# Two rounds of a crowded expert pair, merged tile by tile

## The reference

```python
def hierarchical_moe(h, w_grp, w_exp, w1, w3, w2):
    # t: 256 tokens x 1024
    # top-1 of 4 groups, then top-2 of that group's 4 experts, with weights
    gate = jnp.sum(jax.nn.one_hot(expert, N_EXPERTS, ...) * e_w[..., None], axis=1)
    hg = jnp.einsum('td,edf->tef', t, w1)
    hu = jnp.einsum('td,edf->tef', t, w3)
    a = jax.nn.silu(hg) * hu * gate[..., None].astype(t.dtype)
    y = jnp.einsum('tef,efd->td', a, w2)
```

## Time and profile before

| | |
|---|---|
| median of three executions | 819.1 us |
| the profiled execution: its own time | 825.06 us |
| its span, first to last instruction | 823.3 us |
| TensorE busy | 763.1 us (93%) |
| VectorE, ScalarE, GpSimd busy | 234.7, 165.1, 50.1 us |
| moved by DMA, mean over the span | 289.66 MB, 352 GB/s |
| mean granted TensorE clock | 0.95 of full speed |

### The profile page before, as it was taken

One profiled execution on the slowest core, in us unless ns is written; L12 is line 12 of the kernel. 1 busy time (PEld: TensorE's weight loads), 2 busy tenths in 40 slices (PEclk: granted clock), 3 DMA queues, 4 the chain that ended last, 5 costly groups with the idle time before them and its releaser, 6 DMA issues.

```text
span 823.3 us, 10418 instructions
## 1 busy us (share of the span) xinstructions
PE 763.1 (93%) x4039; PEld 428.6 (52%) x4039; DVE 234.7 (29%) x666; ACT 165.1 (20%) x372; POOL 50.1 (6%) x74
## 2 busy tenths in 40 slices
PE   4799879999999999999899999999997989999796
PEld 4287458764344433443588758683334333333344
DVE  2301331441112111110679931451211112111115
ACT  3120330331000110011503852451000000110012
POOL 5013000010000000000100000001000000001000
PEclk9899999869999999999999999959997999999988
DMA  9996999969999999999997359567999909999941
GB/s 290 400 398 238 413 409 429 361 270 378 425 427 426 425 429 428 425 427 416 399 402 275 112 223 427 195 267 317 431 427 422 398 9 414 426 427 424 424 190 55
DMA packets 42640, 289.66 MB, mean 352 GB/s; under 512 B 4417, under 2 KB 5901, under 8 KB 30290
## 3 DMA queue, kind: packets, MB, share of 16 engines
q1 hardware_dynamic: 36752, 275.78, 81.9%
q0 software_dynamic: 5056, 11.98, 3.9%
q10 hardware_dynamic: 770, 1.06, 0.4%
HBM read 285.63 MB, written 8.52 MB: 357 GB/s over the span
## 4 chain that ended last, share of the span: by engine, by line
PE 79%; DMA 13%; DVE 3%; issue 3%; ACT 1%; POOL 1%; SPq 0%; DVEq 0%; POOLq 0%
PE ps L518 75%; DMA ring<-in_w_ada 6%; DMA ring<-in_conv_w 4%; DMA back<-in_moe_w 4%; DVE work L1753 1%; PE ps L944 1%; PE ps L809 1%; PE ps L742 1%; PE ps L780 0%; DVE rstd L1490 0%; POOL work L1371 0%; PE ps L670 0%; DVE back L1954 0%; PE ps L1064 0%; ACT back L1137 0%
## 5 line engine op out<-in xcount | busy, mean ns | idle before, releaser
L518 PE MATMUL ps<-ring,work 128*64 128x512 f32 x1088 | 306.2, 596 | 2.0 <-DMA back<-in_moe_w 1.1
L518 PEld LDWEIGHTS ps<-ring,work 128*64 128x64 f32 x1088 | 95.0, 137 | 144.1 <-issue 143.8
L518 PE MATMUL ps<-back,ring 128*128 128x256 f32 x656 | 147.4, 386 | 4.3 <-ACT back L1137 3.1
L518 PEld LDWEIGHTS ps<-back,ring 128*128 128x128 f32 x656 | 126.2, 194 | 24.7 <-issue 4.2
L518 PE MATMUL ps<-bench,work 128*64 128x512 f32 x208 | 97.5, 618 | 3.4 <-issue 3.3
L518 PE MATMUL ps<-spare,work 128*64 128x512 f32 x176 | 80.1, 609 | 4.7 <-issue 4.7
L518 PE MATMUL ps<-back,work 128*64 128x512 f32 x160 | 72.0, 596 | 0.0
L1753 DVE TENSOR_TENSOR work<-work,ps 128x256 f32<-128x256 f32 x34 | 19.4, 613 | 161.7 <-PE ps L518 161.7
L518 PE MATMUL ps<-ring,csil 128*32 128x512 f32 x352 | 45.7, 649 | 8.5 <-DMA ring<-in_w_ada 8.5
L1203 ACT ACTIVATE work<-ps 128x512 f32<-128x512 f32 x17 | 10.1, 597 | 210.1 <-PE ps L518 210.1
L1918 DVE SCALAR_TENSOR_TENSOR work<-work,dw 128x256 f32<-128x256 f32 x120 | 50.9, 485 | 1.0
(11 more groups left out here) (238 smaller groups left out, 640.2 us busy)
## 6 DMA issues: line engine op xcount, KB each, us to landing
ring<-in_moe_w SPq DMA_DIRECT2D x63, 2048.0 KB, 19.4
ring<-in_w_ada SPq DMA_DIRECT2D x22, 2048.0 KB, 17.8
bench<-in_moe_w SPq DMA_DIRECT2D x12, 2048.0 KB, 20.3
spare<-in_moe_w SPq DMA_DIRECT2D x11, 2048.0 KB, 20.2
back<-in_moe_w SPq DMA_DIRECT2D x10, 2048.0 KB, 21.2
ring<-in_conv_w SPq DMA_DIRECT2D x6, 2048.0 KB, 24.4
ring<-in_w_in_ab SPq DMA_DIRECT2D x2, 2048.0 KB, 25.0
ring<-in_w_out_ab SPq DMA_DIRECT2D x2, 2048.0 KB, 23.1
```

What stands on the lines that cost most here:

```text
L518: return nc.tensor.matmul(out, lhsT, rhs, start=start, stop=stop, skip_group_check=True)
```

## The change

For a crowded pair of kind 1, the last pair of a layer excepted, the three engines run a new function `both` in the block behind the program. It walks the tiles once: w1 for round 0 (bank 6) and for round 1 (bank 4), then w3 for round 1 (bank 5) and for round 0 (bank 7). The two w1 tiles are given back behind the first product of w3, the two w3 tiles behind round 1's transposes; then come w2 of round 1, the transposes of round 0, the scatter of round 1, the next pair's token rows, and w2 of round 0, behind which w2's tiles are given back. Round 1 has its own scatter matrix, `spread_more`. At the end the engines jump to the next pair (`pe_next`) instead of into the middle of this one; the usual code of the pair is skipped. The usual code now ends with the jump to `pe_next`, where it had one to `pe_round` before it. VectorE's `compact` is split into helpers (`take_spread`, `choose_next`, `gated_rows`, `turned_high`, `give_high`) with the same instructions in the same order. The waits on `ysel_lo`, `ysel_hi`, `hsel_lo` and `hsel_hi` stand behind the second reading of `path` instead of ahead of it. The core of the diff (TensorE, then ScalarE's and VectorE's `both`):

```diff
+        spread_more = work[:, 46 * P:48 * P]
...
+def both(l, i):
+    n = i + l * PAIRS
+    w1, w3, w2 = experts_of(l, i)
+    chosen = (hsel, hsel_more)
+    pe.wait_ge(ysel_lo[0], n)
+    pe.wait_ge(ysel_hi[0], n)
+    pe.wait_ge(hsel_lo[0], n + 1)
+    pe.wait_ge(hsel_hi[0], n + 1)
+    pe.wait_ge(more_ready, n + 1)
+    gather(1, i, 0)
+    gather(1, i, 1)
+    tile_landed(l, i, 0)
+    tile_landed(l, i, 1)
+    pe.wait_ge(mod_taken, (6, 9)[l])
+    for r, bank in ((0, 6), (1, 4)):
+        pe.wait_ge(hsel_lo[r], n + 1)
+        for k in range(DC):
+            if k == 4:
+                pe.wait_ge(hsel_hi[r], n + 1)
+                pe.wait_ge(pick_ready[r], n + 1)
+                if r:
+                    pe.wait_ge(spread_ready[0], n + 1)
+                for g in range(2):
+                    if is_sent(l, i, r):
+                        last = mm(ps[:, 7, 0:4].rearrange("p (s u) -> p s u", s=2), pick[i % 2][:, g, :],
+                                  send[:, g, :, 2 * i:2 * i + 2], g == 0, g == 1)
+                    else:
+                        last = nc.tensor.transpose(ps[:, 7, g * TG:(g + 1) * TG], pick_gate[:, g, :], ident)
+                last.then_inc(spread_done[r], 1)
+            for u in range(2):
+                c = slice(CAP * u, CAP * u + CAP)
+                last = mm(ps[c, bank, :], chosen[r][:, k, c], w1[u][:, k, :], k == 0, k == DC - 1)
+        last.then_inc(hid_done[r], 1)
+    tile_landed(l, i, 2)
+    tile_landed(l, i, 3)
+    for r, bank in ((1, 5), (0, 7)):
+        if r == 0:
+            pe.wait_ge(spread_ready[1], n + 1)
+        for k in range(DC):
+            for u in range(2):
+                c = slice(CAP * u, CAP * u + CAP)
+                last = mm(ps[c, bank, :], chosen[r][:, k, c], w3[u][:, k, :], k == 0, k == DC - 1)
+            if k == 0 and r:
+                pe.wait_ge(hid_done[1], n * 2 + 1)
+                pe.sem_inc(tiles_used, 2)
+        last.then_inc(hid_done[r], 1)
+    def turn(r, bank):
+        for f in range(FC):
+            if f % 2 == 0:
+                pe.wait_ge(hid_ready[r], n * 2 + (f // 2 + 1))
+            last = nc.tensor.transpose(ps[:, bank + f // 2, (f % 2) * P:(f % 2 + 1) * P],
+                                       hid[:, f * P:(f + 1) * P], ident)
+            if f % 2:
+                last.then_inc(turn_done[r], 1)
+    def outer(r):
+        for h in range(2):
+            if r == 0:
+                pe.wait_ge((hsel_lo, hsel_hi)[h][0], n + 2)
+            for f in range(FC):
+                if h == 0 and f % 2 == 0:
+                    pe.wait_ge((hidT_lo[r], hidT_hi[r])[f // 2], n + 1)
+                for u in range(2):
+                    c = slice(CAP * u, CAP * u + CAP)
+                    last = mm(ps[c, 4 + h, :], hidT[:, f, c], w2[u][:, f, h * 512:(h + 1) * 512],
+                              f == 0, f == FC - 1)
+            if h == 0 or not is_sent(l, i, r):
+                last.then_inc(ysel_done[r], 1)
+            else:
+                last.then_inc(tiles_used, 2)
+    def scatter(r, rows):
+        pe.wait_ge(ysel_lo[r], n + 1)
+        for m in range(DC):
+            if m == 4:
+                pe.wait_ge(ysel_hi[r], n + 1)
+            last = mm(psx[:, m, :], ysel[:, m * P:(m + 1) * P], rows, False, True)
+            if m == 0 and r == 0:
+                pe.wait_ge(ysel_done[r], ysel_count(l, i, r) + 2)
+                pe.sem_inc(tiles_used, 2)
+        last.then_inc(round_done[r], 1)
+    turn(1, 4)
+    pe.wait_ge(hid_done[0], n * 2 + 2)
+    pe.sem_inc(tiles_used, 2)
+    tile_landed(l, i, 4)
+    tile_landed(l, i, 5)
+    outer(1)
+    turn(0, 6)
+    pe.wait_ge(y_zeroed, l + 1)
+    scatter(1, spread_more)
+    pe.wait_ge(rows_in, 16 * (i + l * FETCHED + 1))
+    turn_rows(0)
+    if i + 2 < PAIRS:
+        locate(l, i + 2, ps[:, 5, 0:1])
+    pe.wait_ge(at_ready, min(i + 2, FETCHED) + l * FETCHED)
+    turn_rows(1)
+    outer(0)
+    if not is_sent(l, i, 0):
+        scatter(0, spread)
...
         way = pe.value_load(path[0:1, i:i + 1], min_val=0, max_val=2)
         with pe.If(way == 1):
-            pe.wait_ge(more_ready, n + 1)
-            gather(1, i, 0)
-            gather(1, i, 1)
-            compact(l, i, 1)
+            if i + 1 < PAIRS:
+                both(l, i)
+            else:
+                pe.wait_ge(ysel_lo[0], n)
+                pe.wait_ge(ysel_hi[0], n)
+                pe.wait_ge(hsel_lo[0], n + 1)
+                pe.wait_ge(hsel_hi[0], n + 1)
+                pe.wait_ge(more_ready, n + 1)
+                gather(1, i, 0)
+                gather(1, i, 1)
+                compact(l, i, 1)
+                pe.wait_ge(pick_back, n + 1)
+                compact(l, i, 0)
 
             pe.sem_inc(gather_done[2], 2)
             pe.sem_inc(hperm_done, 1)
             pe.sem_inc(gatebc_done, 1)
             pe.sem_inc(dense_done, 2 * FC)
...
-        pe.wait_ge(pick_back, n + 1)
-        pe.wait_ge(hsel_lo[2], n + 1)
-        pe.wait_ge(hsel_hi[2], n + 1)
-        pe.br(f"pe_round_{n}")
+            pe.wait_ge(hsel_lo[2], n + 1)
+            pe.wait_ge(hsel_hi[2], n + 1)
+            compact(l, i, 0)
+        pe.br(f"pe_next_{n}")
...
-        pe.br(f"pe_round_{n}")
-        nc.switch_bb(f"pe_round_{n}", parent=pe_at[n])
         compact(l, i, 0)
+        pe.br(f"pe_next_{n}")
+        nc.switch_bb(f"pe_next_{n}", parent=pe_at[n])
...
+def both(l, i):
+    n = i + l * PAIRS
+    take_low(1, n)
+    act.wait_ge(hid_done[1], n * 2 + 1)
+    nc.scalar.activation(sil, ps[:, 4, :], ACT.Silu).then_inc(sil_ready[1], 1)
+    act.wait_ge(turn_done[1], n * 2 + 1)
+    nc.scalar.activation(hidT[:, 0:2, :], ps[:, 4, 0:2 * P].rearrange("p (f j) -> p f j", f=2),
+                         ACT.Copy).then_inc(hidT_lo[1], 1)
+    act.wait_ge(hid_done[0], n * 2 + 1)
+    act.wait_ge(hid_ready[1], n * 2 + 2)
+    nc.scalar.activation(sil, ps[:, 6, :], ACT.Silu).then_inc(sil_ready[0], 1)
+    act.wait_ge(ysel_done[1], 2 * n + 1)
+    if l == 1:
+        act.wait_ge(y_sent, 16 * min(i, SENT))
+    nc.scalar.activation(ysel[:, 0:512], ps[:, 4, :], ACT.Copy).then_inc(ysel_lo[1], 1)
+    act.wait_ge(turn_done[0], n * 2 + 1)
+    nc.scalar.activation(hidT[:, 0:2, :], ps[:, 6, 0:2 * P].rearrange("p (f j) -> p f j", f=2),
+                         ACT.Copy).then_inc(hidT_lo[0], 1)
+    take_low(0, n + 1)
+    give_low(l, i, 0)
...
+def both(l, i):
+    n = i + l * PAIRS
+    take_high(1, n)
+    take_spread(l, i, 0, spread)
+    dve.wait_ge(more_ready, n + 1)
+    choose_gate(i, pick_ready[1], pick_more)
+    take_spread(l, i, 1, spread_more)
+    choose_next(l, i)
+    gated_rows(l, i, 1, 5)
+    turned_high(l, i, 1, 5)
+    gated_rows(l, i, 0, 7)
+    give_high(l, i, 1)
+    turned_high(l, i, 0, 7)
+    if i + 2 < PAIRS:
+        take_at(l, i + 2, ps[:, 5, 0:1])
+    take_high(0, n + 1)
+    give_high(l, i, 0)
+    dve.sem_inc(pick_back, 1)
```

More of the change, by code:

```diff
@@ L1241, in crowded @@
                     with act.If(way == 1):
-                        take_low(1, n)
-                        compact(l, i, 1)
+                        if i + 1 < PAIRS:
+                            both(l, i)
+                        else:
+                            take_low(1, n)
+                            compact(l, i, 1)
+                            compact(l, i, 0)
                         act.sem_inc(hsel_lo[2], 1)
@@ L1257, in crowded @@
                         take_low(2, n)
-                    act.br(f"act_round_{n}")
+                        compact(l, i, 0)
+                    act.br(f"act_next_{n}")
             def moe_act(l):
@@ L1717, in sum_sent, with take_spread @@
                                 ALU.add).then_inc(y_summed, 1)
-            def compact(l, i, r):
+            def take_spread(l, i, r, rows):
                 n = i + l * PAIRS
@@ L1736, in compact, with choose_next, gated_rows @@
                 else:
[L1737 to L1748, removed]
+                    V.tensor_copy(rows, ps[:, 7, 0:NT]).then_inc(spread_ready[r], 1)
+            def choose_next(l, i):
+                choose_gate(i + 1, pick_ready[0])
+                choose_more(l, i + 1)
+                if i + 2 < PAIRS:
+                    choose_pick(l, i + 2, 0, (picked[0], l * PAIRS + i + 3))
+            def gated_rows(l, i, r, bank):
+                n = i + l * PAIRS
                 dve.wait_ge(sil_ready[r], n + 1)
@@ L1754, in compact, with turned_high, give_high @@
                                     sil.rearrange("s (p f) -> s f p", f=FC)[:, f, :],
-                                    ps[:, 7, :].rearrange("s (p f) -> s f p", f=FC)[:, f, :],
+                                    ps[:, bank, :].rearrange("s (p f) -> s f p", f=FC)[:, f, :],
                                     ALU.mult).then_inc(hid_ready[r], 1)
[L1757 to L1760, removed]
+            def turned_high(l, i, r, bank):
+                n = i + l * PAIRS
                 dve.wait_ge(turn_done[r], n * 2 + 2)
```

(51 more changed lines are left out.)

15 lines of the change are left out of this document (7 added, 8 removed).

## The result

The changed kernel takes 808.38 us (median of four, 807.33 to 811.08); the kernel before, with a fourth execution beside it, 820.04. The ratio is 0.986 with a 95% interval of 0.983 to 0.989: 11.7 us less, where 8.5 were forecast, inside the range. A second comparison gave 0.9856 (0.9828 to 0.9883). The profiled execution of before was a long one (825.06; its other executions on record lie between 815.81 and 823.55), so the spans, 823.3 and 806.3, differ by more than the medians; 2.9 us of that had already arisen ahead of pair 3 (tile 26 goes out at 623.12 instead of 626.03).

A forecast was written before the change was run, and what follows sets the result against it. The weight stream, idle 18.1 us in pair 3, was taken to bound layer 1's end. Waits -6.7, clock -2.2 and TensorE's path +0.4 gave -8.5 us: 819.1 to 810.6, range 807 to 817.5.

The forecast's parts named there:

- Added: End of pair 3: jump into the next pair costs 3.31 + 1.7 us, plus 1.3 for reading `path` and a compare.
- TensorE's sum: TensorE's own path through crowded pair 3: 1.3 - 0.7 - 0.8 + 0.6 = +0.4 us, bounds -1.7 and +3.8.
- the entry: Jump into pair 3's far block: waits partly overlap the second reading of `path`, -0.7 us, at most 0.9.
- The 0.78 ahead of the transposes: Inside pair 3: round 1's transposes no longer wait for VectorE, since round 0's w3 stands between; -0.8 us.
- the new wait for `at_ready`: Right behind `locate` in pair 3: a bare trip to VectorE and back, 0 to 1.2 us, taken as +0.6.
- all three waits go: Pairs 6 and 7: TensorE's waits for tiles, 0.82, 1.14 and 4.71 us, vanish; 6.7 us, plus 2.2 of clock.
- TensorE bounds the rest: End of layer 1: tile 45 lands at 775.7, TensorE wants it at 776.8, so the stream delays nothing further.
- tile 33: Weight stream after pair 3: lands at 710.0, not 717.3; less than 5 us earlier would show the forecast wrong.
- that pass still waits over 2 us: Pair 7's w3 pass: no idle time expected before it; a wait over 2 us would show the forecast wrong.
- the dear exit: End of pair 3: exit costs 6.72 us plus a second stall of 1.85; TensorE loses 5.7, 815.9 us; chance 0.10.
- the late code: Inside `both`: TensorE stops twice more for code at 6.72 us each, 13.4 in all, 824.0 us; chance 0.07.
- shorter waits without a profiler: Last pairs' tile waits: unprofiled, only 2.9 of 8.9 us can go, 2.5 left, 816.6 us; chance 0.10.

The follow-up runs named there:

- the second experiment: Changed kernel with the four tiles of w1 and w3 given back only just ahead of round 0's w2 products: 821.6 us, ratio to before 1.0025.
- the drained kernel: Changed kernel with TensorE waiting for its own last w2 product before the jump to the next pair: 812.2 us, ratio to before 0.988.
- the reversed blocks: Kernel before with only the far blocks of all pairs laid out in reverse order: median 818.0 us, ratio 0.998; traced execution 813.65.
- the scatter last: Changed kernel with round 1's eight scatter products moved behind round 0's w2 products: 802.2 us, repeated 804.9; ratio to before 0.980.

## Why the prediction was right, and where it was not

The direction, the mechanism and the range held. The end of layer 1 was bound by the weight stream, and the gain is the standstill taken out of it: without the early give-backs nothing is left of it (the second experiment), and the time follows "26 to 45" through most of the table (not for the drained kernel, which was late by itself, nor for the reversed blocks, where the trace is not of a typical execution).

The step that failed is the one headed "Added": a jump at the end of the pair, "I price it equally, 3.31 + 1.7", with 1.3 on top. In the changed kernel these 6.3 us are not there. The row of before was read as the price of a jump wherever it stands; it was what was left of it with little work queued ahead. VectorE's copy that the last wait ahead of that jump is for:

```profile
661.65 0.69 DVE L1775 COPY work<-ps 128x512 f32<-128x512 f32 x1 [6.78 <-PE ps L518]
```

It ends at 662.34; the rest of the scatter, 2.8 us, runs behind it, and the next product starts at 668.50, 6.2 us after the copy. In the changed kernel the like copy ends at 676.18, and the products queued behind that wait last until pair 4 starts at 682.73, 6.5 us. Drained, the gap is 3.70 again. So the jump is hidden when enough products stand behind the last wait. How long it takes is not one number in these runs: 6.2 us from the wait in before, 4.6 in the same code with the blocks reversed, 3.70 behind the drain.

The rest of TensorE's sum: the entry was to win 0.7 by overlap and won nothing (3.54 against 3.56), but the gather took 632.80 - 626.25 = 6.55 us instead of 9.02, for the most part because no second stall of 1.85 stood in it; whether that came of the block's new place is open. The 0.78 ahead of the transposes went, but 0.35 came ahead of w2; the new wait for `at_ready` costs 0.25 where 0.6 were set. In all TensorE needed 682.51 - 623.58 = 58.9 us from the last wait's end to w2's give-back, against 694.14 - 626.49 = 67.7, and kept those 8.7 us in pair 4 (w1 back at 690.15; 66.6 against 75.3). Forecast was +0.4.

That carried into the stream. Counted from tile 26's issue, w1 was to come back after 26.7 us, w3 after 41.7, w2 after 62.3 and the next w1 after 76.2; they came after 25.0, 38.7, 59.4 and 67.0. So the stream won 12.8 us, not 7.3. And since TensorE arrived earlier too, "all three waits go" and "TensorE bounds the rest" were wrong: tile 45 still ended last, with 3.02 us of idle time. In the pair of traces: 8.7 on the path, 6.67 - 3.02 = 3.7 of waits, 0.8 of slow clock. Forecast were +0.4 on the path and 8.9 off the waits and their clock; the two errors, 9.1 and 4.4 us, point in opposite ways, so that the total came within 3 us is in part luck. Of the forecast's own signs, tile 27's issue (25.0 us behind tile 26's), the missing gap in mid-pair and tile 33 (13 us earlier) held; the gap at the pair's end did not come, the strip has one dip instead of two, and "that pass still waits over 2 us", named as a sign of being wrong, came true.

Of the rivals, the dear exit fell by its price, the late code by the missing gaps inside `both` (0.35 and 0.25 are the only ones), and shorter waits without a profiler by the medians. The price of a jump that the Trainium skill gives (Advanced Engine Details and Errata, Control Flow Timing) can't be told from a hidden one in the changed kernel, and the drained one shows 3.5 us more than the estimate of 0.16 from its figures. The same page's Engine Queue Depths gives TensorE a queue of 64; that jumps vanish behind queued products agrees with it, though no run here measures the depth.

## What to carry to other kernels

When a stream of loads sets the end, count how long it stands still and who ends each standstill. Here a give-back that came while the queue was still full bought next to nothing, and the last one of the group counted most: moving eight products behind it was worth another 3 to 6 us. Work queued behind the last wait ahead of a jump hid the jump, so put the waits early and plain work last. And hold a trace against the spread of the times before building on its small rows: the second stall was in one trace only.

## What the runs showed of the hardware that was not expected

- TensorE's jump into the far block of pair 3 shows 3.35 to 3.75 us of idle time in every trace, 2.7 of them behind the last wait's end (2.69 in before, 2.67 in the changed kernel). The jump out shows 3.31 us in before, 1.76 with the blocks reversed, 3.70 when drained, and none where products stand queued behind the last wait (6.5 us of them in the changed kernel).
- The 32 gather products took 3.83, 5.44, 6.5 or 7.2 us for the same work: the granted clock behind the entry's gap was 1.00 in the first, 0.68 in the second and 0.51 to 0.57 in the slowest. One kernel, traced twice, had 5.44 and 6.47.
- The read-back of sent rows, four transfers of 512 KB beside the weight tiles, landed up to 28 us after its issue and, with the weights early enough, became what TensorE last waited for (2.56 us with the scatter last).
